# The second layer's MLP in seven block products per pair of weight tiles, instead of eight

## The reference, cut to what matters

```python
def _trunk_layer(x, mod, lp, ctx):
    sh1, sc1, g1, sh2, sc2, g2 = jnp.split(mod, N_MOD, axis=-1)
    h = _rms_norm(x, lp['norm1_g']) * (1 + sc1) + sh1
    proj = h @ lp['w_in']
    ...
    x = x + g1 * mix
    h2 = _rms_norm(x, lp['norm2_g']) * (1 + sc2) + sh2
    x = x + g2 * (jnp.square(jax.nn.relu(h2 @ lp['w_ff1'])) @ lp['w_ff2'])
```

## Time and profile before

| | |
|---|---|
| median of 3 runs | 1905.97 us (1903.74 to 1907.45) |
| the profiled execution, own time | 1910.12 us |
| its span, first to last instruction | 1908.5 us |
| mean granted TensorE clock | 0.987 |
| PE busy | 95% of the span |
| DVE, ACT, POOL busy | 56%, 37%, 24% |
| mean DMA traffic | 97 GB/s |

### The profile page before, as it was taken

How to read it: one execution, slowest core, us unless ns; L and a number is a source line. 1 busy time by engine, 2 the same in 40 slices (tenths; PEclk the granted TensorE clock), 3 DMA queues, 4 the chain that set the end, 5 groups by cost and what they waited for, 6 DMA issues and landing times. The chain is left out here.

```text
span 1908.5 us, 32411 instructions
## 1 busy us (share of the span) xinstructions
PE 1814.3 (95%) x13863; PEld 1722.1 (90%) x13863; DVE 1066.0 (56%) x1639; ACT 705.0 (37%) x1125; POOL 464.3 (24%) x334
## 2 busy tenths in 40 slices
PE   5999999898999999999999999889899999999996
PEld 3899976688999999999999998668899999999995
DVE  3687775567635676767655567556763323323233
ACT  2465346634341231312336533764433223131231
POOL 4000010144441230503530001105444113040244
PEclk9999999999999999999999999999999999999998
DMA  8653130111233444444132223002121221212211
GB/s 350 243 188 104 61 95 9 40 35 62 89 122 138 146 139 163 144 146 153 67 138 74 54 74 102 16 5 70 62 89 67 78 78 67 89 67 68 87 45 55
DMA packets 61147, 184.97 MB, mean 97 GB/s; under 512 B 21957, under 2 KB 34029, under 8 KB 45389
## 3 DMA queue, kind: packets, MB, share of 16 engines
q1 hardware_dynamic: 59468, 181.43, 27.6%
q10 hardware_dynamic: 1536, 1.48, 0.2%
HBM read 174.08 MB, written 8.72 MB: 96 GB/s over the span
## 5 line engine op out<-in xcount | busy, mean ns | idle before, releaser
L1655 PE MATMUL PS<-HH,HI 128*128 128x320 f32 (+1 forms) x1792 | 418.0, 315 | 5.2 <-DVE HL L1095 5.2
L1655 PE MATMUL PS<-HL,HI 128*128 128x320 f32 (+1 forms) x1792 | 413.2, 312 | 0.0
L1655 PE MATMUL PS<-HH,LO 128*128 128x320 f32 (+1 forms) x1792 | 411.1, 311 | 0.0
L713 ACT CAST HI<-RAW 128x2048 fp32r<-128x2048 f32 x96 | 182.7, 1903 | 470.7 <-PE PS L1655 444.1
L1655 PEld LDWEIGHTS PS<-HH,HI 128*128 128x128 f32 x1792 | 301.6, 190 | 5.8 <-issue 5.7
L1655 PEld LDWEIGHTS PS<-HL,HI 128*128 128x128 f32 x1792 | 306.8, 191 | 0.0
L1655 PEld LDWEIGHTS PS<-HH,LO 128*128 128x128 f32 x1792 | 303.9, 190 | 0.0
L1655 PE MATMUL PS<-FH,HI 128*128 128x320 f32 x1280 | 292.4, 310 | 5.5 <-issue 3.5
L1655 PE MATMUL PS<-FH,LO 128*128 128x320 f32 x1280 | 291.4, 309 | 0.0
L1088 DVE TENSOR_TENSOR LO<-RAW,HI 128x2048 fp32r<-128x2048 f32 x96 | 232.7, 2424 | 99.4 <-ACT HI L713 99.3
L1655 PE MATMUL PS<-FL,HI 128*128 128x320 f32 x1152 | 262.3, 309 | 0.0
(11 more groups left out here) (281 smaller groups left out, 2178.3 us busy)
## 6 DMA issues: line engine op xcount, KB each, us to landing
RAW<-ws SPq DMA_DIRECT2D x96, 1024.0 KB, 4.9
WM<-adt SPq DMA_DIRECT2D x48, 512.0 KB, 3.7
ADA<-ada SPq DMA_DIRECT2D x16, 1024.0 KB, 8.1
WMX<-adt SPq DMA_DIRECT2D x16, 512.0 KB, 3.8
EG<-gc SPq DMA_DIRECT2D x20, 256.0 KB, 3.9
X<-xT SPq DMA_DIRECT2D x1, 2560.0 KB, 15.6
X<-xT SPq DMA_DIRECT2D x2, 1280.0 KB, 5.8
xs<-X SPq DMA_DIRECT2D x1, 2560.0 KB, 8.0
```

Of the source, the lines that this page charges most:

```text
L713: nc.scalar.copy(HI[g % 2][:, :], RAW[g % 2][:, :]).then_inc(hi_ready, 1)
L1655: last = pe.matmul(bank(2 * u + a)[:, 0:e], w[:, cols], m[:, a * HT:a * HT + e], start=(k == 0 and f), stop=(k == KT - 1 and e_))
```

## The change

The second layer's MLP is computed as a product of 2 x 2 blocks in seven products in place of eight (Winograd's form of Strassen's method). For a pair `p` of weight tiles, the output is 2 tiles (`m`) x 2 token halves (`a`), and the contraction is cut in two halves of 4 blocks of 128. Each of the seven products is 4 blocks x 3 = 12 matmuls of 320 or 322 columns into one PSUM bank; `w_ff1` gives 16 pairs and `w_ff2` 16, so 224 products and 2688 matmuls.

- Four of the seven weight operands of a pair are sums of blocks. They are made by DMA in DRAM: SP copies 32 blocks of 1 MB in the first layer's MLP, and POOL issues 32 accumulating DMAs of 1 MB, each of which waits for the one before: 16 in the first layer's MLP, 12 before the second layer's rotated keys, 4 in the first four steps of its scan.
- A weight operand is now 128 x 512 (256 KB), loaded into one of eight slots of `RAWB`, rounded by ACT 6 products ahead (`weight_hi`), rest by DVE 5 ahead (`weight_lo`).
- The seven streamed operands of the first product (`HB`, rows of 336) are built while the output projection runs. Those of the second are built from the hidden values: ACT squares, POOL makes four sums (`hidden_sums`), SP stores seven blocks per pair in DRAM (`hb`), loads them back as 7 blocks of 128 x 1280 per four pairs (`block_in`), ACT rounds (`block_split`), DVE or POOL subtracts, four times, just before they are used.
- Results are combined from the banks: ACT copies one (`E1`), DVE adds or subtracts (`sums`, `upper_left`, `lower_right`, `upper_right`, `lower_left`) and multiplies by the norm row straight from PSUM (`scale`).
- In the second half ACT scales, POOL adds to `X`. The last norm turns its row twice; DVE reads it from PSUM for six tiles of `y`, POOL from `RB` for two.

```diff
+                    for w in range(7 * PAIRS7):
+                        if w + SLOTS < 7 * PAIRS7:
+                            sp.wait_ge(F["wlo"], b["wlo"] + w + 1)
+                            weights_in(w + SLOTS)
+                        p, i = divmod(w, PRODUCTS)
+                        if i == 5 and 2 <= p < HALF + 2:
+                            hidden_out(p - 2)
...
+                def weight_sum(l, d):
+
+                    g, kind = divmod(d, 4)
+                    if kind == 0:
+                        pool.wait_ge(sums_copied[g], 80)
+                    if d:
+                        pool.wait_ge(sums_added, 16 * d)
+                    first = l * CHUNKS + 16 + 4 * g
+                    src = blocks_of(first, 4, 2 + kind) if kind < 2 else sums_of(4 * g, 4, kind - 1)
+                    nc.gpsimd.dma_start(sums_of(4 * g, 4, kind), src, accum_op=ALU.add).then_inc(sums_added, 16)
...
+                    if l in FAST:
+                        for d in range(16, 28):
+                            weight_sum(l, d)
...
+                        if l in FAST and s < 4:
+                            weight_sum(l, 28 + s)
...
+                    for w in range(7 * PAIRS7):
+                        p, i = divmod(w, PRODUCTS)
+                        if i == 1:
+                            first_copy(p)
+                        if w in (1, 2):
+                            for j in (2 * w - 2, 2 * w - 1):
+                                act.wait_ge(F["hbt"], b["hbt"] + 3 * H + j + 1)
+                                block_hi(6, j, bank(6 + j % 2)[:, 0:HT])
...
+                        if w + HI_AHEAD < 7 * PAIRS7:
+                            weight_hi(w + HI_AHEAD)
...
+                        if 1 <= p <= HALF and i in (2, 3):
+                            hidden(p - 1, i - 2)
...
+                        if i == 0 and p:
+                            pe.wait_ge(F["c11"], b["c11"] + p)
+                        if i == 1 and p:
+                            pe.wait_ge(F["c12"], b["c12"] + p)
+                        if i == 2 and p:
+                            pe.wait_ge(F["u2"], b["u2"] + p)
+                        if i == 3:
+                            pe.wait_ge(F["e1"], b["e1"] + p + 1)
+                        if i == 4 and p:
+                            pe.wait_ge(F["c21"], b["c21"] + p)
+                        if i == 5:
+                            pe.wait_ge(F["u4"], b["u4"] + p + 1)
+                        if i == 6:
+                            pe.wait_ge(F["c22"], b["c22"] + p + 1)
```

More of the change, by code:

```diff
@@ L77 @@
 MF = 16
+FAST = (1,)
+PAIRS7 = 32
+HALF = PAIRS7 // 2
+PRODUCTS = 7
+SLOTS = 8
+BW = 336
+SHIFTED = (0, 3, 4, 6)
+BX = HT + 2
+HI_AHEAD, LO_AHEAD = 6, 5
 R_ALOG, R_DT, R_SINK = 0, 8, 16
@@ L152, in build @@
         X = place("X", [P, KT, 2, HT], F32, r_x)
-        RAW = [place(f"RAW{i}", [P, KT * CH]) for i in range(2)]
+        r_raw = region(2 * KT * CH * 4)
+        RAW = [place(f"RAW{i}", [P, KT * CH], F32, r_raw + i * KT * CH * 4) for i in range(2)]
+        RAWB = place("RAWB", [P, SLOTS, H * P], F32, r_raw)
         r_split = region(4 * KT * CH * 4)
@@ L288, in halves, with cond @@
             return x[:, k, 0:T].rearrange("p (a b) -> p a b", a=2)
+        def cond(x, g):
+            return x[:, HL_:HT] if g else x[:, 0:HL_]
         def nat(x, g, c=0):
@@ L346, in build, with fast_base, operand, stage @@
         S = {n: sem(n) for n in PER}
+        F = {n: S[x] for n, x in LENT.items()}
+        lent = {x: FPER[n] for n, x in LENT.items()}
         def base(l):
-            return {n: l * c for n, c in PER.items()}
+            n_fast = len([x for x in FAST if x < l])
+            return {n: l * c + n_fast * (lent[n] if n in lent else 0) for n, c in PER.items()}
+        def fast_base(l):
+            return {n: base(l)[x] + PER[x] for n, x in LENT.items()}
+        BANKS = (0, 3, 1, 0, 2, 3, 2)
+        PLAIN = {0: 0, 3: 1, 6: 3}
+        SUMMED = {4: 0, 1: 1, 2: 2, 5: 3}
+        def operand(w):
+            return RAWB[:, w % SLOTS, :]
+        slot_in = mw_in[3:8] + [c_in, k_in, x_in]
+        sums_copied = slot_in
+        def stage(n):
+            return n % 4 if n < PRODUCTS else n % PRODUCTS
+        def stage_turn(n):
+            return len([x for x in range(n) if stage(x) == stage(n)])
+        STARTS = (0, 2, 0, 1)
+        def blocks_of(g, n, part):
+            return t["ws"][g:g + n, 32 * part:32 * part + 32, :].rearrange("p r c -> r p c")
+        def sums_of(p, n, kind):
+            return t["wp"][kind, p:p + n].rearrange("p r c -> r p c")
+        VECTOR_BLOCKS, POOL_BLOCKS = (0, 1, 3, 4, 6), (2, 5)
+        STORED = (0, 3, 4, 1, 5, 2, 6)
         def decays(i):
@@ L559, in _, with square_sum @@
             def _(pool):
-                def square_sum(n, x):
+                def square_sum(n, x, tmp=None, ks=range(KT)):
                     c = 15 * n
-                    for k in range(KT):
+                    tmp = TC[0][:, 0:T] if tmp is None else tmp
+                    for k in ks:
                         t_ = x(k)
@@ L1072, in _ @@
                     done(7)
-                root(4)
+                act.wait_ge(nss, 5)
+                nc.scalar.activation(RT[:, 0:NB], bank(4)[:, 0:NB], ACT.Sqrt, bias=eps, scale=1.0 / D).then_inc(nrt, 1)
+                act.wait_ge(nrb, 6)
+                nc.scalar.copy(flat(RB[:, :, :]), pair(3)).then_inc(nrd, 1)
             @block.vector
@@ L1586, in next_mod @@
                         mod_tile(n, n - MF, WM[n % 3], CB)
+                    if l in FAST:
+                        fast_mlp(l, residual)
+                        continue
                     q = 2 * l + 1
@@ L1629, in _ @@
                             dve.wait_ge(S["moda_done"], o["moda_done"] + 2)
-                root(4)
-                for k in range(5):
+                dve.wait_ge(nrt, 5)
+                nc.vector.reciprocal(RT[:, 0:NB], RT[:, 0:NB]).then_inc(nrr, 1)
+                dve.wait_ge(nrb, 5)
+                for k in range(6):
                     dve.wait_ge(y_fg, k + 1)
-                    nc.vector.tensor_tensor(YB[:, k, :, :], YB[:, k, :, :], RB[:, :, :], ALU.mult).then_inc(y_rb[0], 1)
+                    y = flat(YF[:, k, :, :])
+                    nc.vector.tensor_tensor(y, y, pair(2), ALU.mult).then_inc(y_rb[0], 1)
             @block.tensor
```

494 lines of the change are left out of this document (474 added, 20 removed).

## The result

Four runs of the changed kernel on one chip gave 1888.65 us in the median (1884.68 to 1890.82), four of the kernel before 1904.88 (1903.74 to 1907.45): ratio 0.9903, interval [0.9891, 0.9915], or 16.2 to 20.8 us less. The forecast was 43.7 less. It is faster, by about 1%, and by less than half of what was forecast.

A forecast was written before the change was run, and what follows sets the result against it. The second layer's MLP was taken as bound by PE's matmul count. Terms -56.3 + 5.5 + 5.6 + 3.0 - 2.0 + 0.5 = -43.7 us took 1905.97 to 1862.3 us, range 1850 to 1873.

The forecast's parts named there:

- matmul count: Second MLP: 224 products of 12 matmuls, 394.9 us, replace 64 tiles, 451.2 us; -56.3 us if PE never waits.
- steady first half: Second MLP's steady pairs: DVE, ACT and POOL fit within the 12.35 us of a pair, so PE waits 0.
- start of the MLP: Start of the second MLP: waits for the last feature block, ACT's copy and DVE's queue, +5.5 us, bounds 0 and 12.
- first transition: First change from first to second product: 4.1 us of waits, 5.6 with DVE's rests slowed by POOL.
- other three transitions: The later three changes between products: without relu and scalings 1.0 us each, +3.0 in all.
- scan and all ahead of the MLP: Before the second MLP: accumulating DMAs hidden at 10 us each; their issue in the scan costs +0.5 us, bound 4.
- the end: After the last product: POOL's square +1.0, last tile ready 3.0 earlier; net -2.0 us.
- rival A: Second MLP: small waits in each pair from queue order, POOL beside DVE or DMA; 0.7 us per pair, 1884; chance 0.22.
- Rival B: Weight sums: slow accumulating DMAs make POOL late to the keys; at 22 us each 1930; chance 0.12.
- the slowing: Transitions: POOL slows DVE's 1280-column rests, taking the first from 4.1 to 5.6 us, the others to 1.0 each.
- the 0.3: Later three transitions: 0.3 us of waits each before POOL's slowing, with relu and scalings gone.
- Rival C: Second MLP: waits between products lower PE's clock; at 0.84 throughout, 470 us for 395, 1937; chance 0.04.

The follow-up runs named there:

- E1: Not a run: the copy of one result bank that ACT makes in the changed kernel; no measured time is given for it.
- no_blocks: Changed kernel without the rounding and subtraction of all 28 hidden blocks (outputs differ); second MLP 407.80 us against 434.55.
- gates_only: Changed kernel with DVE gating from PSUM from pair 16 on, without ScalarE's scaling and POOL's residuals; second MLP 429.60 us against 434.55.
- gates_slices: As gates_only, with POOL's block subtraction also cut into four slices; second MLP 422.10 us against the changed kernel's 434.55.
- combo_dve: As combo_slices, but DVE subtracts all seven hidden blocks and POOL none; timed 1876.19 us, ratio to before 0.9837, second MLP 424.66 us.
- start_order: Changed kernel with four early DVE weight rests moved behind the residuals of feature blocks 6 and 7; second MLP 430.94 us against 434.55.
- combo_slices: gates_slices and start_order together on the changed kernel; timed 1871.59 us, ratio to before 0.9814, second MLP 421.31 us.
- tail_psum: Changed kernel with the last pair's c22, c12 and c21 left in PSUM; from last MLP matmul to the end 19.0 us against 20.5.

## Why the prediction was wrong in size

The terms, with what the trace of after gives for each (2688 matmuls at the 147.56 ns that no_blocks shows in 2628 without a gap are 396.6 us; the norm's 1.5 stay):

| term | forecast | measured |
|---|---|---|
| matmul count | -56.3 | -55.8 |
| steady first half | 0 | +0.7 |
| start of the MLP | +5.5 | +9.2 |
| first transition | +5.6 | +9.2 |
| other three transitions | +3.0 | +17.1 |
| scan and all ahead of the MLP | +0.5 | -0.9 |
| the end | -2.0 | -1.1 |
| sum | -43.7 | -21.6 |

The last column is of the profiled execution, whose own difference from the output projection on is 21.4.

**The count** was right, pitch and all: one bank instead of two costs nothing (1417 matmuls in 207.66 us in no_blocks are 146.5 ns each, 146.7 before), and some 100 hand-overs in the first half cost 0.7 us together. **The steady state** was right too (in pair 3 DVE is busy 9.1 us and ACT 7.6 of 12.4, forecast 9.2 and 8.3; the terms given for ACT add up to 8.2), and rival A fell there; DMA at 0.77 to 0.83 of its engines holds nothing up. A's time, 1884, was near the result by luck: it named POOL beside DVE, but the waits are at the transitions and not in each pair. **Rival B** fell: the accumulates land in 10.3 and 9.8 us, as taken. The Trainium skill ("DMA: Bandwidth & Descriptors", Anatomy of one DMA) gives a fit for a DMA from GpSimd, from which I estimate 4.4 us for 1 MB; the traces have no plain one from GpSimd, and the accumulating ones take more than twice that.

**The step that failed** is "The other three times relu and scalings are gone, and I find 0.3 and the same slowing: 1.0 each". They cost 5.7 each. Two things were wrong in it, the slowing and the 0.3. I took the slowing as some tenths of each rest, from rows of 640 columns beside POOL. But the rows of after show a wait for the end of POOL's instruction, and that instruction is the block of 3.1 to 3.75 us which the change itself gives POOL. I had costed POOL's two blocks as its own time, 3.4 each, and not as time taken from DVE at the moment when DVE had least to spare. The runs show this: with fewer pieces on POOL (gates_only) and smaller ones too (gates_slices) the stops fall from 3.74 to 2.80 and 1.72, while DVE's own work rises by 2 us per pair; slices alone bring only 0.2, or 1.1 against the 4.67 at full clock. The Trainium skill ("SBUF — State Buffer", Who interferes with whom) states it: a DVE instruction with two SBUF inputs contends with a GpSimd instruction that reads SBUF, and it calls the pair of ports that they share an exclusive lock. The trace agrees: the 2.74 us became 0.68 with one operand in PSUM.

The 0.3 was wrong too, and that part is DVE's own load, which my layout had too small: with POOL silent and all seven blocks on DVE (combo_dve) 2.07 stay, and DVE has no idle time there. What the five blocks of the changed kernel would leave without POOL's hold no run shows.

Of the 17.1, 11.2 are visible stops and most of the rest matmuls at the lower clock. But start_order shows that PE would have waited for the blocks in that time anyway: the clock's own part is about 0.8 of the 17.1, in the last transition. Rival C was a mechanism of this kernel at a small scale. The Trainium skill ("TensorE: Matmul & The Clock Gate", A second HAM failure mode) tells of a throughput degraded by such a cost between bursts; in these traces it was 1.3 us for one place of combo_slices, and nothing for two places where PE had a wait ahead of it.

**The first transition** was mis-sized, 9.2 for 5.6. The stops that I laid out by hand come to 6.8 for the 5.6 I gave, and not in the places I gave (I had block 6 at 0.7, it is 1.45; block 4's 2.76 I did not have). The rest is lower clock by the look of it, but start_order, at full clock there, is only 0.4 shorter.

**The start** has the waits that I named, and one more: product 1 waited 3.13 us for the residual of block 7, because DVE was about 4 us behind with four rests ahead of it; I began DVE's account at the end of the last output tile as if it were free then. The next 21 matmuls took 1.5 us longer, at a granted 0.69, but PE waited 2.62 for DVE's reciprocal behind them, so this is no separate loss. **The end**: DVE's six tiles take 4.47 us (4.9 forecast), but PE waits 6.92 us for the norm sums where it was 4.11; that is 2.8 more, not 1.0. tail_psum shows 1.4 of it to be DVE beside POOL.

## What to carry to other kernels

Work that is given to POOL is paid by DVE when both have their operands in SBUF: add the length of POOL's instruction to the path of the DVE instruction beside it, give POOL short instructions at such a place, and keep one of DVE's operands in PSUM. When a change replaces much of one engine's work, account for the few pairs where a stage changes by order, from the moment when each queue really gets there. Don't add slow matmuls behind a stop to the stops: ask first whether PE would have waited there at full clock. A look at one kernel without the suspected work (here 407.8 against 434.6 us) bounds a cause at once.

## What the runs showed of the hardware

- A DVE subtraction of 512 columns from SBUF takes 0.68 us alone and up to 3.43 beside POOL's subtraction of 1280 columns; that of POOL takes 2.95 to 3.75 whole, and in four slices 1.26 to 1.39 each, over 5 us in sum: slices cost POOL 1.5 to 1.7 times as much and still made the kernel shorter.
- Stops of the same length didn't always bring the lower clock: after 3.13 us PE ran 48 matmuls at 1.00 in one kernel and at 0.80 in another (7.49 and 8.80 us), and after 3.4 us ten us at 1.00 and at 0.86, the second pair without a difference in the time of 288 matmuls (43.87 and 43.88 us).
- Accumulating 1 MB from DRAM to DRAM lands in 10 us, a plain copy of 1 MB from DRAM to DRAM by SP in 8.2, and both ran beside PE at no cost (300.00 of 300 us busy at 0.83 of the DMA engines).
